# Two-block transformer on one core: order of VectorE's work in the first layer, and half a weight unit more held ahead of the experts

## The chip, the cores and the metric

The kernel runs on one core of one Trainium2 chip. Its time is the device time of one execution in microseconds (us), given as the median of three executions. The trace comes from one further execution. The engines are TensorE (PE, its weight loads are PEld), VectorE (DVE), ScalarE (ACT), GpSimd (POOL) and SyncE (SP), which here issues nearly all transfers from device memory.

## The reference, cut to what matters

All tensors are float32, with 256 tokens of 1024 channels. Two blocks follow each other, and each has two layers. The first layer of the first block (the "even layer") computes attention and a state-space model (SSM) from one projection:

```python
proj = h @ w_in                       # 1024 x 5120
q, k, v, g_att, u_ssm, g_ssm = split(proj)
lam_bar = exp(lam * dt)               # complex, 32 groups x 64 states
states = scan(a_r * s_l + s_r)        # over the 256 tokens
y = real(c_mat @ states) + d_skip * u_ssm
```

Both layers of the second block end in sixteen experts. Every expert picks its 32 tokens:

```python
xn = rms_norm(h, norm2_g)
affinity = softmax(xn @ w_router)
gate, idx = top_k(affinity.T, 32)     # per expert
xe = xn[idx]
hid = silu(xe @ w_gate) * (xe @ w_up) # 32 x 1024 @ 1024 x 1024
ye = (hid @ w_down) * gate
h = h + scatter_add(ye, idx)
```

The weights of one expert are three matrices of 4 MB, 12 MB in all. One layer of experts reads 201 MB, two read 403 MB of the 514 MB that the program reads.

## The kernel before

**Units.** Weights come in units of 2 MB, 16 KB in each of 128 partitions. SP issues one DMA for each in a fixed order, on one queue, and waits before each until the memory it goes to is free. TensorE counts finished units in `unit_done`. A dense weight is multiplied in three products of rounded parts: ACT copies a landed unit to its high part (`high_part`, L866), DVE subtracts that to get the low part (`low_part`, L1220, 128x4096 elements), and only then may TensorE start the unit (L1635 to L1637). Unit numbers in the text are those of this list: the even layer's are 0 to 10.

**Even layer.** TensorE runs each unit in four quarters, and a table written out by hand (`SSM_STEPS`) puts pieces of the SSM ahead of certain quarters. T0 to T3 (L1792, L1795) build the blocks within four tokens and stand ahead of the third and fourth quarter of unit 3. V0 to V3 (L1807) are the drives of the four groups of states. V2 stands ahead of the second quarter of unit 4, V3 ahead of its fourth. V2 writes the bank that the first group's drive was read from, so it waits until DVE's `states(0)` has read it (the second instruction of `states`, L1197). V3 waits in the same way for `states(1)`. DVE has its own written order: after the powers (`cpow_ready`, a memset at L1265) come `low_part(4)`, eight `whole_block` (L1272, they read what T0 and T1 made), the angles (L1280 to L1291: turns, fractions and the step table), `states(0)`, `low_part(5)`, `states(1)`, and eight more `whole_block`. T2 and T3 reuse the banks of T0 and T1 and wait for the first and the second four `whole_block`. ACT takes the sines of the angles (`sincos`, L825) between the high parts of units 4 and 5. POOL rotates q and k meanwhile (L689 to L694).

**Experts.** An expert is six units: j = 0 to 3 are gate and up, 4 and 5 are down (96 in a layer). There are six places in `ring` and four in `board`. Nine of them form a wheel, and the tenth takes the unit j = 9 (`ONCE`) alone. So ten units are asked for before the first one has been used. Of the unit j = 10 (`HALVED`), the first half (1 MB) goes to `row_half` early. The second half goes to the place of unit j = 0, so it waits until TensorE has done that unit (L615). From then on SP waits for one finished unit ahead of each transfer.

**Ahead of the experts.** The router's scores come to DVE and ACT at the end of each layer's output projection. ACT takes the exponentials (`lg_exp`, L1054). DVE multiplies `x` by 1/rms into `xs` (the first token tile in `normalise(0)`, the second at L1520), finds the 32 best tokens of each expert (L1524 to L1529), and compares the ranks with 0 to 31 (L1532) for `csel`, a one-hot matrix of the first expert. TensorE's `gather` (L2157) multiplies `csel` by `xs` to pick the rows, and DVE's `choose` (L1561) makes `csel` for the expert after the next.

Of the kernel before, what the change touches and what calls it, by code (L numbers as in the profile page):

```python
# [26 lines left out]
ALU = mybir.AluOpType  # L27
# [3 lines left out]
P = 128  # L31
S = 256
D = 1024
NT = S // P
# [19 lines left out]
ONCE = WHEEL  # L54
HEAD_E = 2

HALVED = 10
# [3 lines left out]
def wheel_place(j):  # L61

    return j if j < ONCE else (j - ONCE - 1) % WHEEL


def extra_slot(j):

    return EXTRA - 1 if j == ONCE else EXTRA_OF.get(wheel_place(j))
# [105 lines left out]
def build(nc, a, out):  # L174

    with ExitStack() as ctx:
# [21 lines left out]
        row = row_half[:, 0:D]  # L198
        vec = sb("vec", [P, NVEC])
# [136 lines left out]
        csel = next_area("p (i c) -> p i c", i=NT, c=CAP)  # L336
        wselT = next_area("p (i s) -> p i s", i=NT, s=P)
# [64 lines left out]
        user, place, high_place, slot_no, count_in, loads = [], [], [], [], [], [0] * (RING + EXTRA)  # L402
# [165 lines left out]
        half_in = sem("half_in")  # L568
# [18 lines left out]
        def _(sp):  # L587
# [13 lines left out]
            for l in range(2):  # L601
# [6 lines left out]
                def load_moe(e, j, turn=None):  # L608
# [5 lines left out]
                    elif j > ONCE:  # L614
                        sp.wait_ge(unit_done, u - (WHEEL if j - ONCE > WHEEL else WHEEL + 1) + 1)  # L615
# [8 lines left out]
                    if turn is None and j == HALVED:  # L624
                        src = down[e, :, 1, :, :].rearrange("p b n -> p (b n)")
                        sp.dma_start(slot_mem(s)[:, SLOT // 2:SLOT], src).then_inc(landed[s], 16)
                        return
# [21 lines left out]
                for j in range(6 * (HEAD_E + TURN_E)):  # L649
                    if j not in (2, 3):  # L650
                        load_moe(j // 6, j)
                    if j == 1:
                        sp.wait_ge(rot_done, 8 * (l + 1))
                        sp.dma_start(row_half[:], down[HALVED // 6, :, 0, :, :].rearrange("p b n -> p (b n)")).then_inc(half_in, 16)
# [416 lines left out]
        def _(dve):  # L1071
# [203 lines left out]
            low_part(4)  # L1275
            for t in range(8):
                whole_block(t)
# [16 lines left out]
            own.settle()  # L1294
            states(0)
            low_part(5)
            states(1)
# [91 lines left out]
            for l in range(2):  # L1389
# [119 lines left out]
                normalise(0)  # L1509
# [22 lines left out]
                tt(csel, slot_in[:, :, 0:1].to_broadcast([P, NT, CAP]), cn("slots").unsqueeze(1).to_broadcast([P, NT, CAP]),  # L1532
                   ALU.is_equal).then_inc(csel_sb, 1)
# [83 lines left out]
        def _(pe):  # L1617
# [351 lines left out]
            for l in range(2):  # L1969
# [178 lines left out]
                count["xs"] += 2 * NT  # L2148

                def gather(e):  # L2150

                    if isinstance(e, int) and e == 0:
                        pe.wait_ge(xs_ready, count["xs"])
# [15 lines left out]
                def expert(e, j0, turn=None, more=True):  # L2169
# [33 lines left out]
                    for j in range(2):  # L2203
                        w = in_place(4 + j)
                        for qq in range(2):
                            for b in range(2):
                                q = 2 * j + qq
                                ahead_half = turn is None and j0 + 4 + j == HALVED and qq == 0
                                if ahead_half and b == 0:
                                    pe.wait_ge(half_in, 16 * (l + 1))  # L2210
                                if not more and j == 1 and qq + b > 0:
                                    pe.wait_ge(tail_in[2 * qq + b - 1], 16 * (l + 1))
                                for r in range(4):
                                    at = qq * 2 * FF + b * FF + 256 * r
# [80 lines left out]
```

## Time and profile before

| | us |
|---|---|
| median of 3 executions | 1670.78 |
| lowest, highest | 1669.49, 1671.78 |
| profiled execution, its own time | 1668.02 |
| span of its trace | 1666.1 |

The span runs from the first to the last instruction, and 1.9 us of the profiled execution's time lie around it. TensorE is busy for 1315.2 us of the span (79%), DVE for 560.9, ACT for 453.5 and POOL for 125.8. The granted TensorE clock is 0.931 of full speed over the span. The DMA engines move 516.56 MB. In the forty slices of the page one slice is 41.7 us: the first eleven are the first block, then come the second block's two layers, each a dense stretch and a stretch of experts (from about 600 to 1033 us, and from about 1222 to 1656 us).

### The profile page before, as it was taken

To read this page: it belongs to the slowest core of one execution; us is meant where nothing else is said; L and a number is where in the kernel's file an instruction comes from. 1 tells how busy PE (TensorE), PEld (TensorE's weight loads), DVE (VectorE), ACT (ScalarE), POOL (GpSimd) and SP (SyncE) were. 2 spreads that over 40 slices of the span, in tenths; PEclk is the share of its full clock that TensorE was granted. 3 is DMA by queue.
4 is the path that set the end of the run, shared out by engine and by line. 5 is a ranking of instruction groups with operands and counts; after the bars stand their busy time and mean duration, and the time that the engine had idled before them with its cause. 6 is when DMAs were issued, how large, how long until landed. Compare 5 with 4: busy or idle time off the path is not lost.

```text
span 1666.1 us, 28296 instructions
## 1 busy us (share of the span) xinstructions
PE 1315.2 (79%) x12544; PEld 925.8 (56%) x12544; DVE 560.9 (34%) x810; ACT 453.5 (27%) x581; POOL 125.8 (8%) x152
## 2 busy tenths in 40 slices
PE   7999999999999987666656565999987666566664
PEld 6888877998888853323223223788853222233222
DVE  7993675355576530000000001485520000000001
ACT  5346555443654311100001011554311101001011
POOL 0320000000305000000000000305000000000000
PEclk9999999999999999988988887999999888988887
DMA  8234343464444799999999999444899999999997
GB/s 284 102 127 141 126 162 125 169 217 168 152 152 178 308 406 423 426 428 424 428 424 428 426 424 410 144 145 179 331 403 424 425 427 426 427 424 427 426 426 310
DMA packets 87104, 516.56 MB, mean 310 GB/s; under 512 B 6513, under 2 KB 6641, under 8 KB 54513
## 3 DMA queue, kind: packets, MB, share of 16 engines
q1 hardware_dynamic: 83520, 509.20, 75.3%
q0 software_dynamic: 992, 3.42, 0.6%
q10 hardware_dynamic: 2512, 2.75, 0.5%
q8 instruction: 66, 1.08, 0.3%
q14 instruction: 14, 0.11, 0.0%
HBM read 514.30 MB, written 1.05 MB: 309 GB/s over the span
## 4 chain that ended last, share of the span: by engine, by line
DMA 46%; PE 39%; DVE 9%; issue 2%; ACT 2%; SPq 2%; DVEq 0%; ACTq 0%
DMA board<-in_w_gate 12%; DMA board<-in_w_down 11%; DMA ring<-in_w_gate 10%; PE dense L1635 8%; PE dense L1637 8%; PE dense L1636 8%; DMA ring<-in_w_down 6%; DMA ring<-in_w_up 5%; PE bank L2185 3%; PE bank L2215 2%; DVE ring_parts L1220 1%; SPq L637 1%; DVE board L1444 1%; PE dense L1688 1%; PE dense L1652 1%
## 5 line engine op out<-in xcount | busy, mean ns | idle before, releaser
L2185 PE MATMUL bank<-ring,board 128*32 128x256 f32 x2624 | 199.5, 458 | 147.1 <-DMA ring<-in_w_up 85.8
L2185 PEld LDWEIGHTS bank<-ring,board 128*32 128x32 f32 x2624 | 91.8, 126 | 248.6 <-DMA ring<-in_w_up 105.3
L1220 DVE TENSOR_TENSOR ring_parts<-ring,ring_parts 128x4096 fp32r<-128x4096 f32 (+1 forms) x44 | 184.5, 4198 | 104.8 <-ACT ring_parts L866 104.6
L1058 ACT ACTIVATE board<-bank 128x256 f32<-128x256 f32 x32 | 12.3, 385 | 740.6 <-PE bank L2185 740.6
L1551 DVE TENSOR_TENSOR board<-board,bank 128x256 f32<-128x256 f32 x32 | 13.5, 422 | 555.9 <-ACT board L1058 555.9
L866 ACT ACTIVATE ring_parts<-ring 128x4096 fp32r<-128x4096 f32 (+1 forms) x48 | 165.1, 3441 | 125.4 <-DMA ring<-in_w_in 39.3
L2185 PE MATMUL bank<-board 128*32 128x256 f32 x1472 | 105.6, 439 | 65.9 <-DMA board<-in_w_up 40.5
L1635 PE MATMUL dense<-board_parts,ring_parts 128*128 128x256 f32 x528 | 152.2, 288 | 0.0
L1637 PE MATMUL dense<-board_parts,ring_parts 128*128 128x256 f32 x528 | 149.4, 283 | 0.0
L1635 PE MATMUL dense<-ring_parts,board_parts 128*128 128x512 f32 x320 | 128.5, 401 | 0.0
L1636 PE MATMUL dense<-ring_parts,board_parts 128*128 128x512 f32 x320 | 124.8, 390 | 0.0
L2215 PE MATMUL bank<-ring,board 128*32 128x256 f32 x1312 | 85.5, 405 | 49.3 <-DMA ring<-in_w_down 42.9
L2185 PEld LDWEIGHTS bank<-board 128*32 128x32 f32 x1472 | 49.4, 123 | 120.3 <-DMA board<-in_w_up 51.3
L1636 PE MATMUL dense<-board_parts,ring_parts 128*128 128x256 f32 x400 | 113.1, 283 | 0.0
L1637 PE MATMUL dense<-ring_parts,board_parts 128*128 128x512 f32 x272 | 106.1, 390 | 0.0
L1635 PEld LDWEIGHTS dense<-board_parts,ring_parts 128*128 128x128 f32 x528 | 101.2, 192 | 1.2 <-issue 0.9
L1637 PEld LDWEIGHTS dense<-board_parts,ring_parts 128*128 128x128 f32 x528 | 101.2, 192 | 0.0
L730 POOL TENSOR_TENSOR board<-board 128x128 f32<-128x128 f32 x64 | 24.3, 400 | 914.0 <-PE bank L2193 772.3
L2215 PEld LDWEIGHTS bank<-ring,board 128*32 128x32 f32 x1312 | 41.3, 115 | 85.9 <-DMA ring<-in_w_down 52.0
L1556 DVE COPY board<-bank 128x256 f32<-128x256 f32 x32 | 13.6, 425 | 221.1 <-PE bank L2215 221.1
L1636 PEld LDWEIGHTS dense<-board_parts,ring_parts 128*128 128x128 f32 x400 | 76.7, 192 | 0.5 <-issue 0.2
L2215 PE MATMUL bank<-board 128*32 128x256 f32 x704 | 48.5, 421 | 28.7 <-DMA board<-in_w_down 25.1
(338 smaller groups left out, 2066.4 us busy)
## 6 DMA issues: line engine op xcount, KB each, us to landing
ring<-in_w_gate SPq DMA_DIRECT2D x42, 2048.0 KB, 40.8
ring<-in_w_up SPq DMA_DIRECT2D x40, 2048.0 KB, 40.8
ring<-in_w_down SPq DMA_DIRECT2D x40, 2048.0 KB, 40.9
board<-in_w_up SPq DMA_DIRECT2D x24, 2048.0 KB, 41.1
board<-in_w_gate SPq DMA_DIRECT2D x22, 2048.0 KB, 41.0
board<-in_w_down SPq DMA_DIRECT2D x20, 2048.0 KB, 40.9
ring<-in_w_in SPq DMA_DIRECT2D x18, 2048.0 KB, 7.9
ring<-in_even_w_in SPq DMA_DIRECT2D x10, 2048.0 KB, 8.3
```

The source lines that it names most:

```text
L637: sp.dma_start(dst, src).then_inc(tail_in[n - 1] if n else landed[s], 16)
L730: g.tensor_tensor(wsel[:, i], csel[:, i:i + 1, :].to_broadcast([P, 4, CAP]), aff[:, i, bass.ds(e, 1)].unsqueeze(2).to_broadcast([P, 4, CAP ...
L866: s.activation(slot_of(u, True)[0], slot_of(u), ACT.Copy).then_inc(hi_done, 1)
L1220: tt(lo, slot_of(u), hi.bitcast(F32), ALU.subtract).then_inc(lo_done, 1)
L1444: tt(qv, qv, by, ALU.mult).then_inc(lv_ready, 1)
L1635: mm(o, x_parts[0], y_parts[0], start=start, stop=False)
L1636: mm(o, x_parts[0], y_parts[1], start=False, stop=False)
L1637: return mm(o, x_parts[1], y_parts[0], start=False, stop=stop)
L1652: last = mm(d[:, i, :], act_T[:, k, i, :], w[:, k, :], start=k == 0, stop=k == nk - 1)
L1688: last = mm(d[:, c // 2, (c % 2) * S:(c % 2 + 1) * S], w[:, k, c * P:(c + 1) * P], act_T[:, k, :], start=k == 0, stop=k == nk - 1)
L2185: last = mm(WB[0][32 * q:32 * q + 32, 256 * (j % 2):256 * (j % 2) + 256], xeT[:, 4 * (j // 2) + k, :], w[:, k * D + 256 * q:k * D + 256 * ...
L2215: last = mm(WB[3][32 * r:32 * r + 32, 0:256], hidT[:, b, 32 * q:32 * q + 32], (row_half if ahead_half else w)[:, at:at + 256], start=q == ...
```

## The change

Four things change, none of them in what is computed.

1. In the even layer DVE's order becomes: angles, eight `whole_block`, `low_part(4)`, `states(0)`, `states(1)`, `low_part(5)`, then as before.
2. The gather reads `x` instead of `xs`. The 1/rms is put into the one-hot matrix: `cselr` is `csel` with `rstd` in place of the ones. The normalisation of `x` into `xs` ahead of the experts goes.
3. The memory of `xs` (1 MB) is free then, and takes the second half of unit j = 10, from the moment that the router's exponentials are done. Unit j = 11 is now the first on the wheel, and waits for unit j = 0; the units 11 to 18 each wait for the unit one earlier than before, 19 for one two earlier, and those from 20 on wait as before.
4. `choose` makes `cselr` as well as `csel`, with one instruction more for each token tile.

```diff
-HALVED = 10
+ONCE, HALVED = WHEEL, WHEEL + 1
 def wheel_place(j):
-    return j if j < ONCE else (j - ONCE - 1) % WHEEL
+    return j if j < ONCE else (j - HALVED - 1) % WHEEL
 def extra_slot(j):
-    return EXTRA - 1 if j == ONCE else EXTRA_OF.get(wheel_place(j))
+    return {ONCE: EXTRA - 1, HALVED: EXTRA}.get(j, EXTRA_OF.get(wheel_place(j)))
...
+        half_mem = [row_half[:], xs[:].rearrange("p i n -> p (i n)")]
...
-                    elif j > ONCE:
-                        sp.wait_ge(unit_done, u - (WHEEL if j - ONCE > WHEEL else WHEEL + 1) + 1)
+                    elif j > HALVED:
+                        sp.wait_ge(unit_done, u - (WHEEL if j - HALVED > WHEEL else WHEEL + 2) + 1)
...
-                    if j not in (2, 3):
+                    if j not in (2, 3, HALVED):
                         load_moe(j // 6, j)
-                    if j == 1:
-                        sp.wait_ge(rot_done, 8 * (l + 1))
-                        sp.dma_start(row_half[:], down[HALVED // 6, :, 0, :, :].rearrange("p b n -> p (b n)")).then_inc(half_in, 16)
+                    if j in (1, ONCE):
+
+                        sp.wait_ge(*((rot_done, 8 * (l + 1)) if j == 1 else (lg_exp, 2 * (l + 1))))
+                        n = int(j == ONCE)
+                        sp.dma_start(half_mem[n], down[HALVED // 6, :, n, :, :].rearrange("p b n -> p (b n)")).then_inc(half_in[n], 16)
...
-            low_part(4)
-            for t in range(8):
-                whole_block(t)
             turns = lambda f: cs[:, f, :].rearrange("p (t b) -> p t b", t=SSM_TILES)
...
             own.settle()
+            for t in range(8):
+                whole_block(t)
+            low_part(4)
             states(0)
+            states(1)
             low_part(5)
-            states(1)
             for t in range(8, SSM_TILES):
                 whole_block(t)
...
-                normalise(0)
+                inverse(0)
...
-                ts(xs[:, 1, :], x[:, 1, :], rstd[:, 1:2], None, ALU.mult).then_inc(xs_ready, 2)
...
-                tt(csel, slot_in[:, :, 0:1].to_broadcast([P, NT, CAP]), cn("slots").unsqueeze(1).to_broadcast([P, NT, CAP]),
-                   ALU.is_equal).then_inc(csel_sb, 1)
+                own.link(tt(csel, slot_in[:, :, 0:1].to_broadcast([P, NT, CAP]),
+                            cn("slots").unsqueeze(1).to_broadcast([P, NT, CAP]), ALU.is_equal))
+                tt(cselr, csel, rstd[:].unsqueeze(2).to_broadcast([P, NT, CAP]), ALU.mult).then_inc(csel_sb, 1)
...
                     dve.wait_ge(wsel_sb, e * 2 + 2 * NE * l)
+                    for i in range(NT):
+                        stt(cselr[:, i, :], cn("slots"), slot[:, i, bass.ds(e, 1)], rstd[:, i:i + 1].to_broadcast([P, CAP]),
+                            ALU.is_equal, ALU.mult)
...
-                            last = mm(WB[3][32 * q:32 * q + 32, 256:512].rearrange("p (b m) -> p b m", b=2), csel[:, i, :],
-                                      xs[:, i, :].rearrange("p (m q b) -> p q b m", q=4, b=2)[:, q], start=i == 0,
+                            last = mm(WB[3][32 * q:32 * q + 32, 256:512].rearrange("p (b m) -> p b m", b=2), cselr[:, i, :],
+                                      x[:, i, :].rearrange("p (m q b) -> p q b m", q=4, b=2)[:, q], start=i == 0,
```

VectorE in the even layer, from the end of the powers (L1265). Before, the low part of unit 4 (L1220) comes first, then the eight blocks (L1272), then the angles (from L1280):

```order
L1265 MEMSET stat 128x1
L1220 TENSOR_TENSOR ring_parts<-ring,ring_parts 128x4096
L1272 SCALAR_TENSOR_TENSOR xs<-con,skip,bank 128x128 x8
L1280 TENSOR_TENSOR board<-con,row_half 128x1024
L1282 TENSOR_SCALAR board<-board 128x1024
L1283 TENSOR_SCALAR row_half<-board 128x1024
```

And now, the same place (the angles are L1277 to L1288):

```order
L1265 MEMSET stat 128x1
L1277 TENSOR_TENSOR board<-con,row_half 128x1024
L1279 TENSOR_SCALAR board<-board 128x1024
L1280 TENSOR_SCALAR row_half<-board 128x1024
L1281 TENSOR_SCALAR board<-board 128x1024
L1282 TENSOR_SCALAR row_half<-row_half 128x1024
L1283 TENSOR_SCALAR board<-board 128x1024
L1284 TENSOR_TENSOR board<-board,row_half 128x1024
L1286 TENSOR_TENSOR board<-board 128x1024
L1288 TENSOR_TENSOR row_half<-row_half,con 128x1024
L1272 SCALAR_TENSOR_TENSOR xs<-con,skip,bank 128x128 x8
L1220 TENSOR_TENSOR ring_parts<-ring,ring_parts 128x4096
```

The low part of unit 4 has moved behind the angles and the blocks.

VectorE at the end of `states(0)` (L1208, L1209). Before, the low part of unit 5 stands between it and `states(1)` (from L1196):

```order
L1208 TENSOR_TENSOR board<-board 128x256
L1209 TENSOR_TENSOR board<-board 128x256
L1220 TENSOR_TENSOR ring_parts<-ring,ring_parts 128x4096
L1196 TENSOR_TENSOR board<-bank,board 128x512
L1197 TENSOR_TENSOR board<-bank,board 128x512
L1200 TENSOR_TENSOR board<-board 128x256
```

And now:

```order
L1208 TENSOR_TENSOR board<-board 128x256
L1209 TENSOR_TENSOR board<-board 128x256
L1196 TENSOR_TENSOR board<-bank,board 128x512
L1197 TENSOR_TENSOR board<-bank,board 128x512
L1200 TENSOR_TENSOR board<-board 128x256
L1201 TENSOR_TENSOR board<-board 128x256
L1204 SCALAR_TENSOR_TENSOR board<-row_half,board 128x256 x2
L1206 TENSOR_TENSOR board<-board 128x512
L1207 TENSOR_TENSOR board<-board 128x512
L1208 TENSOR_TENSOR board<-board 128x256
L1209 TENSOR_TENSOR board<-board 128x256
L1220 TENSOR_TENSOR ring_parts<-ring,ring_parts 128x4096
```

`states(1)` follows `states(0)` at once, and the low part of unit 5 comes after both.

SyncE ahead of the experts. Before, from the unit j = 7 on; the row of 128x2048 elements is the second half of unit j = 10:

```order
L643 DMA ring<-in_w_up 128x4096
L643 DMA ring<-in_w_gate 128x4096
L643 DMA board<-in_w_up 128x4096
L626 DMA ring<-in_w_down 128x2048
L643 DMA ring<-in_w_down 128x2x2048
L643 DMA board<-in_w_gate 128x4096
```

And now:

```order
L641 DMA ring<-in_w_up 128x4096
L641 DMA ring<-in_w_gate 128x4096
L641 DMA board<-in_w_up 128x4096
L654 DMA xs<-in_w_down 128x2048
L641 DMA ring<-in_w_down 128x2x2048
L641 DMA ring<-in_w_gate 128x4096
```

The half unit keeps its place in the queue, but goes to `xs`, and its wait is for the exponentials instead of for unit j = 0.

## Rows read from the trace of the kernel before

**Rows 1.** The page: the chain that ended last, by engine.
```profile
DMA 46%; PE 39%; DVE 9%; issue 2%; ACT 2%; SPq 2%; DVEq 0%; ACTq 0%
```

**Rows 2.** Stretches: busy us of each engine (count), then granted clock, DMA share, GB/s.
```profile
604.50:612.50 8.00, 7.74 (x120) 3.98 (x112) 0.85 (x2) 0.85 (x3) 0.25 (x1) 1.00 0.84 306
612.50:1031.00 418.50, 269.66 (x3470) 129.72 (x3474) 25.73 (x73) 36.64 (x63) 11.11 (x30) 0.88 1.01 425
1226.50:1234.50 8.00, 7.91 (x124) 4.05 (x115) 0.85 (x2) 0.67 (x3) 0.15 (x1) 1.00 0.89 286
1234.50:1652.00 417.50, 271.70 (x3462) 130.24 (x3466) 26.00 (x73) 36.70 (x64) 11.81 (x31) 0.87 1.01 425
```

**Rows 3.** Timeline of TensorE, 77 to 98 us: start, us, engine, line, idle before.
```profile
77.00 0.28 PE L1792 MATMUL bank<-con,xs 128*32 128x32 f32 x3
...
83.48 0.39 PE L1635 MATMUL dense<-ring_parts 128*128 128x512 f32 x1
...
86.25 2.00 PE L1807 MATMUL bank<-board 128*128 128x64 f32 x16
...
96.21 2.00 PE L1807 MATMUL bank<-board 128*128 128x64 f32 x16 [2.43 <-DVE board L1197]
98.02 0.48 PE L1635 MATMUL dense<-ring_parts 128*128 128x512 f32 x1
```

**Rows 4.** Timeline of VectorE, 65 to 96 us.
```profile
65.77 0.06 DVE L1265 MEMSET stat<- 128x1 f32 x1
68.81 4.42 DVE L1220 TENSOR_TENSOR ring_parts<-ring,ring_parts 128x4096 fp32r<-128x4096 f32 x1 [2.98 <-ACT ring_parts L866]
73.15 2.18 DVE L1272 SCALAR_TENSOR_TENSOR xs<-con,skip,bank 128x128 f32<-128x128 f32 x8
75.25 1.22 DVE L1280 TENSOR_TENSOR board<-con,row_half 128x1024 f32<-128x1024 f32 x1
...
84.91 0.69 DVE L1196 TENSOR_TENSOR board<-bank,board 128x512 f32<-128x512 f32 x1
...
90.53 4.42 DVE L1220 TENSOR_TENSOR ring_parts<-ring,ring_parts 128x4096 fp32r<-128x4096 f32 x1
94.87 0.68 DVE L1196 TENSOR_TENSOR board<-bank,board 128x512 f32<-128x512 f32 x1
95.47 0.68 DVE L1197 TENSOR_TENSOR board<-bank,board 128x512 f32<-128x512 f32 x1
```

**Rows 5.** Timeline of GpSimd: first rotation of q, beside L1220 and beside L1272.
```profile
69.78 3.79 POOL L689 TENSOR_TENSOR rtmp<-board,con 128x128 f32<-128x128 f32 x1 [56.78 <-ACT board L787]
73.53 0.45 POOL L690 TENSOR_TENSOR rtmp<-board,con 128x128 f32<-128x128 f32 x1
```

**Rows 6.** Timeline of VectorE, `states(2)`, beside the rotation of k.
```profile
111.71 1.63 DVE L1204 TENSOR_TENSOR_SCAN board<-row_half,board 128x256 f32<-128x256 f32 x2
```

**Rows 7.** Timeline of SP's queue at the start of the experts.
```profile
590.56 0.33 SPq L643 DMA_DIRECT2D board<-in_w_up  x1
604.67 0.33 SPq L626 DMA_DIRECT2D ring<-in_w_down  x1
```

**Rows 8.** Stretches of half a microsecond behind the issue at 604.67.
```profile
604.50:605.00 0.50, 0.50 (x16) 0.32 (x12) 0.00 (x0) 0.00 (x0) 0.00 (x0) 1.00 0.24 98
...
607.00:607.50 0.50, 0.50 (x16) 0.31 (x12) 0.00 (x0) 0.00 (x0) 0.00 (x0) 1.00 1.05 442
```

**Rows 9.** Timeline of VectorE and TensorE ahead of the first gather.
```profile
592.26 0.75 DVE L1520 TENSOR_SCALAR xs<-x,rstd 128x1024 f32<-128x1024 f32 x1
...
598.71 0.23 DVE L1532 TENSOR_TENSOR board<-bank,con 128x64 f32<-128x64 f32 x1 [0.39 <-PE bank L2146]
...
599.09 0.65 PE L2157 MATMUL bank<-xs,board 128*32 128x256 f32 x4 [0.41 <-DVE board L1532]
```

**Rows 10.** Timeline: `choose(1)` on VectorE, and the gather that reads it.
```profile
602.54 0.21 DVE L1561 TENSOR_TENSOR board<-board,con 128x64 f32<-128x64 f32 x1
609.61 2.02 PE L2157 MATMUL bank<-xs,board 128*32 128x256 f32 x16
```

More of the change, by code:

```diff
@@ L51 @@
 TURN_E = 3
-ONCE = WHEEL
+ONCE, HALVED = WHEEL, WHEEL + 1
 HEAD_E = 2
-HALVED = 10
 EXTRA_OF = {2: 2, 3: 1, 4: 0}
 def wheel_place(j):
-    return j if j < ONCE else (j - ONCE - 1) % WHEEL
+    return j if j < ONCE else (j - HALVED - 1) % WHEEL
 def extra_slot(j):
-    return EXTRA - 1 if j == ONCE else EXTRA_OF.get(wheel_place(j))
+    return {ONCE: EXTRA - 1, HALVED: EXTRA}.get(j, EXTRA_OF.get(wheel_place(j)))
 SLOT = 4096
@@ L336, in build @@
         csel = next_area("p (i c) -> p i c", i=NT, c=CAP)
+        cselr = next_area("p (i c) -> p i c", i=NT, c=CAP)
         wselT = next_area("p (i s) -> p i s", i=NT, s=P)
@@ L401, in build @@
         LAST_X = 10
-        user, place, high_place, slot_no, count_in, loads = [], [], [], [], [], [0] * (RING + EXTRA)
+        user, place, high_place, slot_no, count_in, loads = [], [], [], [], [], [0] * (RING + EXTRA + 1)
         extras = []
@@ L567, in build @@
         final_done = sem("final_done")
-        half_in = sem("half_in")
+        half_in = [sem(f"half_in{n}") for n in range(2)]
         tail_in = [sem(f"tail_in{n}") for n in range(3)]
@@ L623, in load_moe @@
                         sp.wait_ge(unit_done, free_at(place[u]))
[L624 to L627, printed above, removed]
                     j = j % 6
@@ L2147, in _ @@
                 last.then_inc(slot_ps, 1)
-                count["xs"] += 2 * NT
                 def gather(e):
-                    if isinstance(e, int) and e == 0:
-                        pe.wait_ge(xs_ready, count["xs"])
                     pe.wait_ge(csel_sb, e + (NE * l + 1))
@@ L2203, in expert @@
                     for j in range(2):
-                        w = in_place(4 + j)
+                        halves = turn is None and j0 + 4 + j == HALVED
+                        w = None if halves else in_place(4 + j)
                         for qq in range(2):
@@ L2207, in expert @@
                                 q = 2 * j + qq
-                                ahead_half = turn is None and j0 + 4 + j == HALVED and qq == 0
-                                if ahead_half and b == 0:
-                                    pe.wait_ge(half_in, 16 * (l + 1))
+                                if halves and b == 0:
+                                    pe.wait_ge(half_in[qq], 16 * (l + 1))
                                 if not more and j == 1 and qq + b > 0:
@@ L2213, in expert @@
                                 for r in range(4):
-                                    at = qq * 2 * FF + b * FF + 256 * r
+                                    at = (0 if halves else qq * 2 * FF) + b * FF + 256 * r
                                     last = mm(WB[3][32 * r:32 * r + 32, 0:256], hidT[:, b, 32 * q:32 * q + 32],
-                                              (row_half if ahead_half else w)[:, at:at + 256], start=q == 0 and b == 0, stop=q == 3 and b == 1,
+                                              (half_mem[qq] if halves else w)[:, at:at + 256], start=q == 0 and b == 0, stop=q == 3 and b == 1,
                                               skip_group_check=True)
```

## The prediction

> **What bounds the kernel now.** I read the chain of waits first. It is 46% transfers, 39% TensorE and 9% VectorE [rows 1]: the kernel has dense stretches, where TensorE sets the time, and expert stretches, where the weights do. So each part of the change has to be valued by the bound of its own stretch.
>
> In the expert stretches the table of windows shows 425 GB/s over 418.5 and 417.5 us, and TensorE busy for about 65% of them [rows 2]. The transfers are the bound there, and a microsecond in which they stand still before the stretch ends is lost for good. Just ahead of each of these windows there are 8 us with only 306 and 286 GB/s [rows 2]. At 425 GB/s those bytes need 8 x 306/425 = 5.8 us and 8 x 286/425 = 5.4 us: 2.2 and 2.6 us are lost there. The reason stands in SP's queue. The last of the ten units asked for in advance is issued at 590.56, the next transfer waits for TensorE's first unit and is issued at 604.67 [rows 7]. By then the queue has run dry: 98 GB/s right behind the issue, and 442 only at 607.0 [rows 8].
>
> In the even layer I looked for places where TensorE stands still. In the stretch that the change touches there is one: V3 (L1807 at 96.21) waited 2.43 us for DVE's L1197 [rows 3]. DVE had begun `states(1)` at 94.87, behind the low part of unit 5, which began at 90.53 [rows 4].
>
> The profiled execution took 1668.02 us, of which 1666.1 are span. The median is 1670.78. I work out a difference from the trace and take it off both.
>
> **Part 1, the even layer.** The same instructions run in another order, so I lay DVE's durations end to end, from the rows of VectorE [rows 4]:
> - Powers end at 65.83. DVE then stood idle for 2.98 us, for ACT's high part of unit 4. The angles need nothing of ACT's and take 84.91 - 75.25 = 9.66 us: they end at 75.5.
> - Eight blocks, 75.25 - 73.15 = 2.10 us: 77.6. The first four are done at 76.5, and T2 is due at 77.00 [rows 3]: 0.5 us to spare.
> - `low_part(4)`, 94.87 - 90.53 = 4.34 us: 81.9. Unit 4 is due on TensorE at 83.48 [rows 3]: 1.5 us to spare.
> - `states(0)`, 90.53 - 84.91 = 5.62 us: 87.6. Its L1197 ends 1.3 us in, at 83.2, and V2 is due at 86.25.
> - `states(1)`: 93.2. Its L1197 ends at 88.9. V3 is due at 96.21 - 2.43 = 93.78: the wait of 2.43 us is gone, with 4.9 us to spare.
> - `low_part(5)`: 97.5, 3 us later than before. Unit 5 is due at V3's start plus V3 (98.02 - 96.21 = 1.81) plus a quarter (86.25 - 83.48 = 2.77): 93.78 + 4.58 = 98.4. This is what is late next, with 0.8 us to spare.
>
> Behind that DVE waits for ACT, which waits for TensorE, and all moves up together. So the gain is 2.4 us. The bounds are 2.5 from one side (the whole wait and a little from V2, which had no slack: L1197 of `states(0)` had ended at 84.91 + 1.3 = 86.2 and V2 began at 86.25) and 0.5 from the other (the next rival). I take 2.4.
>
> **Part 2, half a unit more ahead.** The half (1.05 MB) needs 1.05/0.425 = 2.46 us of the queue. It is now issued once the exponentials are done, which was before 592.26 [rows 9], some 12 us before the queue runs dry. What is left to move after the restart is 1.05 MB less. So the stretch would end 2.46 us earlier if the restart came at the same time.
>
> The restart still waits for TensorE's first unit, and this comes later by the new multiply for `cselr`. The nearest row is L1532, 128x64 elements in 0.23 us [rows 9], and it must wait for `csel` to be written: 0.25 us between L1532 and the gather at 599.09. I charge 0.25, with bounds of 0.2 and 0.5. Gain: 2.46 - 0.25 = 2.2 us in each layer of experts. A cap is the time lost in the dip, 2.2 and 2.6 us, which allows it. The queue would now run dry at 604.5 + 2.46 = 607.0, and what is issued at 604.9 flows from about 607.0 by the same delay as before [rows 8]: it meets just so. If a remnant of the dip stays, 0.5 us goes. Bounds for each layer: 2.5 and 1.2.
>
> Here a page of the Trainium skill can be weighed. "DMA: Bandwidth & Descriptors", section "Latency and other measured facts", puts the first byte of a transfer issued by SyncE about 0.6 us behind its issue. The rows show 98 GB/s right behind the issue and the full rate 2.3 us behind it, so the measurement decides. By the page's figure no remnant could stay, since the new transfer would have 1.5 us in hand; the sum would be the same 2.2, and the lower bound would move up to it.
>
> **Edits that I cost at nothing.** The normalisation of the first token tile lay while DVE had idle time, and L1520 (0.75 us, [rows 9]) while the affinities were being transposed; the chain that follows starts at the same time, give or take 0.1 us. The gather reads `x` in the pattern in which it read `xs`, so it costs the same. `choose` gets two more small instructions for each expert. The nearest row is L1561, 0.21 us, at 602.54, and the gather that needs it is at 609.61 [rows 10]: some 6.9 us of cover where TensorE is the bound, and more later, when it waits for weights. Uncovered, two of them would cost 0.42 us for each of 32 experts, 13.4 us in all. The rotated wheel makes the next layer's first dense units wait for one expert unit more. They still stand behind undelivered weights in the queue, so this costs nothing.
>
> **Sum.** 2.4 + 2.2 + 2.2 = 6.8 us: 1668.0 - 6.8 = 1661.2 for a profiled execution like this one, and 1670.8 - 6.8 = 1664.0 for the median.
>
> **Rivals.**
> - *The wait moves to unit 5 (15%).* DVE works from 65.8 to 97.5 without a pause, and the end has 0.8 us to spare. POOL rotates q in this time. Beside L1220 its first instruction took 3.79 us, beside the blocks 0.45 [rows 5]; and the two scans of `states(2)` took 1.63 us beside POOL [rows 6]. For it: with L1220 now later, the rotation can end inside `states(0)`. If that stretches DVE by 1.5 to 2.7 us, unit 5 starts 0.7 to 1.9 us late, and the even layer gives 0.5 to 1.7 instead of 2.4: 1665.3 at 1.1. Against it: only one or two of POOL's twelve instructions should be left. The Trainium skill speaks for this rival: "SBUF — State Buffer", section "SBUF: two separate sides", has the port pair shared by VectorE and GpSimd as an exclusive lock, so that the other fully blocks. The rows of POOL agree with that.
> - *The dip stays (15%).* The queue runs dry anyway, and the slow start behind it comes again, so that each layer gives 1.0 instead of 2.2: 1670.8 - 2.4 - 2.0 = 1666.4. For it: the meeting at 607.0 has no slack. Against: the bytes are moved ahead in any case.
> - *The half unit doesn't help (4%).* It would do this if TensorE, not the weights, set the pace after the restart. Then only part 1 is left: 1668.4. Against it stands the steady 425 GB/s with TensorE at 65% [rows 2].
> - *Slower (3%).* `choose` comes onto the path. Its place is between the input of one expert and the gather of the next. It decides from the point at which DVE ends `choose` later than TensorE reaches that gather, so when the 6.9 us of cover are used up, and from there each expert pays its 0.42 us: 1670.8 - 6.8 + 13.4 = 1677.4. Nothing in the rows comes near that point.
>
> **How the numbers follow.** The forecast holds 63%: 1664.0, and with the bounds of its terms (0.4 less in the even layer, 0.5 less in each layer of experts; 0.7 more in all) 1663.3 to 1665.4. The first two rivals lie at 1665.3 and 1666.4. The median of three differs by about 1 us from one set to another (1669.49 to 1671.78 before). So the range is 1661.8 to 1668.0, and leaves out the last two rivals and the tails. 0.2%, or 3.3 us, is about what a measurement of this kernel can tell from no change. Faster by more than that: the forecast, nearly all of the first rival, most of the second, 0.88 in all. Within it: the third, the rest of the second, 0.09. Slower: 0.03.
>
> **What would show it.** In the even layer: no idle time ahead of V3, DVE without a pause from the powers to the second eight blocks, and unit 5 not waiting for L1220. If unit 5 waits, the first rival holds. In the experts: the transfer into `xs` issued near 590 us (the even layer's gain already taken off), no stretch of 98 GB/s at the restart, and the 8 us around it near 400 GB/s. The gather 0.25 us later behind L1528 than it was behind L1529. The last weight lands about 2.2 us earlier in the first layer of experts, beyond the even layer's gain, and about 4.4 us in the second. I am wrong if the dip is filled and the end doesn't move, since then the transfers are not the bound that I take them for.

## The result, and the profile after

| | us |
|---|---|
| changed kernel, median of 4 executions | 1661.13 (1660.33 to 1663.90) |
| kernel before, 4 executions beside them | 1670.48 (1669.49 to 1671.78) |
| ratio, 95% interval | 0.9948 [0.9936, 0.9960] |
| predicted | 1664.0, range 1661.8 to 1668.0 |

The change saves 9.35 us where 6.8 were predicted, and the time lies 0.7 us below the range. Two more comparisons of the same kernel (below) gave 0.9936 and 0.9944. The mean of the three ratios is 0.9943, or 9.6 us. The interval of this first comparison (6.7 to 10.7 us) still just takes in the forecast of 6.8. The intervals of the two others do not (8.4 to 12.9 and 7.0 to 11.7), so the gain was too small in the prediction, and this is hardly chance. One execution of before in the sets below took 1885 us at a granted clock of 0.69, and is left out of the comparisons.

The profiled execution of the changed kernel took 1663.90 us. That is only 4.1 less than the profiled execution of before (1668.02), less than half of what the medians show. Before's was 2.5 under its median, this one is 2.8 above its own. It began late: the powers end at 68.1 instead of 65.8 [rows 4]. In its trace TensorE stands idle for 2.16 us ahead of them, within the small matmuls of L1765 (here L1768), without a wait that the profile shows ("issue"):

```profile
38.34 0.31 PE L1768 MATMUL bank<-board,con 32*32 32x64 f32 x7 [2.16 <-issue]
```

The trace of before has no such gap. So I read steps in these two traces, and sizes in the medians.

The chain of waits of the changed kernel (the page):

```profile
DMA 45%; PE 43%; DVE 8%; issue 2%; ACT 2%; SPq 0%; DVEq 0%; ACTq 0%
```

SP's 2% have gone from it [rows 1]. TensorE in the even layer, by timeline (start, us, engine, line, idle before):

```profile
89.33 1.89 PE L1810 MATMUL bank<-board 128*128 128x64 f32 x16
96.61 1.89 PE L1810 MATMUL bank<-board 128*128 128x64 f32 x16
98.31 0.48 PE L1638 MATMUL dense<-ring_parts 128*128 128x512 f32 x1
```

V3 (at 96.61) has no idle time ahead of it, where it had 2.43 us [rows 3]. VectorE in the same stretch:

```profile
68.00 1.22 DVE L1277 TENSOR_TENSOR board<-con,row_half 128x1024 f32<-128x1024 f32 x1
...
76.58 2.16 DVE L1272 SCALAR_TENSOR_TENSOR xs<-con,skip,bank 128x128 f32<-128x128 f32 x8
78.65 4.42 DVE L1220 TENSOR_TENSOR ring_parts<-ring,ring_parts 128x4096 fp32r<-128x4096 f32 x1
82.99 0.69 DVE L1196 TENSOR_TENSOR board<-bank,board 128x512 f32<-128x512 f32 x1
...
84.38 0.67 DVE L1200 TENSOR_TENSOR board<-board 128x256 f32<-128x256 f32 x1
...
89.72 0.68 DVE L1197 TENSOR_TENSOR board<-bank,board 128x512 f32<-128x512 f32 x1
90.51 0.43 DVE L1200 TENSOR_TENSOR board<-board 128x256 f32<-128x256 f32 x1
...
94.73 4.42 DVE L1220 TENSOR_TENSOR ring_parts<-ring,ring_parts 128x4096 fp32r<-128x4096 f32 x1
```

This is the chain that the prediction laid end to end, without a pause, 2.2 us later at its start and 1.6 us at its end. The angles take 76.58 - 68.00 = 8.6 us instead of the 9.66 that were read from the trace of before. L1197 of `states(1)` ends at 90.4, 6.2 us ahead of V3. The low part of unit 5 ends at 99.15, and unit 5 is due a quarter (2.77 us, the prediction's figure) behind 98.31, so 1.9 us later. The first rival's stretching shows, but is small: `states(0)` takes 89.11 - 82.99 = 6.1 us instead of 5.6 [rows 4], since some of its instructions run beside GpSimd: its L1200 takes 0.67, and that of `states(1)` takes 0.43.

The start of the experts, in windows of 8 us around the restart of the queue and then the stretches behind them (columns as in [rows 2]), changed kernel:

```profile
604.00:612.00 8.00, 8.00 (x124) 4.18 (x116) 0.84 (x2) 0.57 (x2) 0.00 (x0) 1.00 0.96 373
1224.00:1232.00 8.00, 8.00 (x140) 4.33 (x132) 0.42 (x1) 0.38 (x1) 0.00 (x0) 1.00 0.97 382
612.00:1029.00 417.00, 272.57 (x3479) 130.34 (x3482) 30.10 (x101) 36.95 (x64) 11.32 (x30) 0.87 1.01 425
1232.00:1650.00 418.00, 269.90 (x3486) 130.81 (x3484) 30.62 (x102) 37.09 (x64) 11.92 (x31) 0.88 1.00 424
```

306 and 286 GB/s have become 373 and 382, and the steady rate stays at 425. What the dip loses falls from 2.2 and 2.6 us to 8 - 8 x 373/425 = 1.0 and 0.8 us. Another profile of the same kernel (the run "the changed kernel again" below) has still less of it:

```profile
602.30:610.30 8.00, 7.98 (x124) 3.88 (x116) 0.85 (x2) 0.60 (x2) 0.01 (x1) 1.00 1.01 423
1220.90:1228.90 8.00, 7.96 (x124) 4.09 (x116) 0.85 (x2) 0.63 (x2) 0.10 (x1) 1.00 1.02 420
```

The stretch ahead of the first gather, first SP's queue and then VectorE and TensorE:

```profile
591.30 0.33 SPq L654 DMA_DIRECT2D xs<-in_w_down  x1
604.45 0.38 SPq L641 DMA_DIRECT2D ring<-in_w_down  x1
```

```profile
598.05 0.23 DVE L1531 TENSOR_TENSOR board<-bank,con 128x64 f32<-128x64 f32 x1 [0.39 <-PE bank L2149]
598.31 0.23 DVE L1533 TENSOR_TENSOR board<-board,rstd 128x64 f32<-128x64 f32 x1
...
598.59 0.67 PE L2157 MATMUL bank<-x,board 128*32 128x256 f32 x4 [0.58 <-DVE board L1533]
```

The half unit is asked for 13 us ahead of the restart. From the start of the making of `csel` to the gather it was 0.38 us [rows 9], and is 0.54 now: `cselr` costs 0.16 us, not 0.25.

### The profile page after: what moved, and what is told of

Same layout as the page of the kernel before. It is cut to its first block, busy times and chain, and to the rows that moved or that the text cites. A ratio compares the mean times of both kernels' runs of the same rounds, so it can differ in the third digit from the quotient of the medians.

```text
span 1662.1 us, 28385 instructions
## 1 busy us (share of the span) xinstructions
PE 1315.4 (79%) x12544; PEld 928.1 (56%) x12544; DVE 567.2 (34%) x866; ACT 453.8 (27%) x581; POOL 125.2 (8%) x152
## 3 DMA queue, kind: packets, MB, share of 16 engines
HBM read 514.30 MB, written 1.05 MB: 310 GB/s over the span
## 4 chain that ended last, share of the span: by engine, by line
DMA 45%; PE 43%; DVE 8%; issue 2%; ACT 2%; SPq 0%; DVEq 0%; ACTq 0%
DMA board<-in_w_down 21%; DMA board<-in_w_gate 15%; PE dense L1638 9%; PE dense L1640 8%; PE dense L1639 8%; DMA board<-in_w_up 5%; PE bank L2185 4%; PE bank L2215 3%; DMA ring<-in_w_up 2%; DVE ring_parts L1220 1%; DMA ring<-in_even_w_in 1%; PE dense L1655 1%; DVE board L1444 1%; DVE board L1435 1%; PE bank L2010 1%
## 5 line engine op out<-in xcount | busy, mean ns | idle before, releaser
L2185 PE MATMUL bank<-ring,board 128*32 128x256 f32 x2688 | 211.2, 470 | 152.2 <-DMA ring<-in_w_up 90.5
L1220 DVE TENSOR_TENSOR ring_parts<-ring,ring_parts 128x4096 fp32r<-128x4096 f32 (+1 forms) x44 | 184.3, 4193 | 105.2 <-ACT ring_parts L866 105.1
L2185 PE MATMUL bank<-board 128*32 128x256 f32 x1408 | 101.2, 440 | 60.1 <-DMA board<-in_w_up 35.5
L2215 PE MATMUL bank<-ring,board 128*32 128x256 f32 x1280 | 77.3, 383 | 50.0 <-DMA ring<-in_w_down 44.7
L1638 PE MATMUL dense<-ring_parts 128*128 128x512 f32 (+1 forms) x192 | 67.8, 353 | 1.3 <-DVE ring_parts L1220 1.3
```

The lines of the kernel that those rows point to most:

```text
L1220: tt(lo, slot_of(u), hi.bitcast(F32), ALU.subtract).then_inc(lo_done, 1)
L1638: mm(o, x_parts[0], y_parts[0], start=start, stop=False)
L2185: last = mm(WB[0][32 * q:32 * q + 32, 256 * (j % 2):256 * (j % 2) + 256], xeT[:, 4 * (j // 2) + k, :], w[:, k * D + 256 * q:k * D + 256 * ...
L2215: last = mm(WB[3][32 * r:32 * r + 32, 0:256], hidT[:, b, 32 * q:32 * q + 32], (half_mem[qq] if halves else w)[:, at:at + 256], start=q == ...
```

## The experiments

All ratios are to the kernel before, run beside on the same chip, five rounds each, with 95% intervals. Three sets of four kernels each had their own executions of before: median 1670.56 for the first four, 1669.52 for the next four (the kernel before again, the filled wait, only `states(1)` moved, the half unit late), 1670.44 for the last four. Gains in us are worked out from the ratio, and can differ by about 1 us from the difference of the medians.

**The even layer's order alone.** The kernel before, with only the new order of VectorE:

```diff
-            low_part(4)
-            for t in range(8):
-                whole_block(t)
...
+            for t in range(8):
+                whole_block(t)
+            low_part(4)
             states(0)
-            low_part(5)
             states(1)
+            low_part(5)
```

> The kernel before with VectorE's new order in the even layer alone (angles, blocks, low part of unit 4, both first states, low part of unit 5). Theory A (the forecast's terms are right, and what was measured beyond 6.8 us is spread between executions): 2.4 us faster than before, ratio 0.9986, and no idle time ahead of V3. Theory B (the even layer's term is mis-sized and holds the missing 2.5 us): 4 to 5 us faster. Theory C (the experts' terms hold it): 2.4 us faster here as well, so A and C are told apart by the run with the experts' part alone.

Measured: 1665.90 us, 0.9970 [0.9961, 0.9979], 5.0 us less (3.5 to 6.5). The forecast of 2.4 lies below the interval.

**The experts' part alone.** The changed kernel, with before's order in the even layer:

```diff
+            low_part(4)
+            for t in range(8):
+                whole_block(t)
...
-            for t in range(8):
-                whole_block(t)
-            low_part(4)
             states(0)
-            states(1)
             low_part(5)
+            states(1)
```

> The changed kernel with VectorE's old order in the even layer, so that only the experts' part is changed. Theory A: 4.4 us faster than before (2.2 in each layer of experts). Theory B: the same 4.4. Theory C: 6 to 7 us faster, more than the 2.46 us a layer that the half unit takes on the queue, so something beside the moved bytes gains.

Measured: 1666.12 us, 0.9977 [0.9968, 0.9987], 3.8 us less (2.2 to 5.3). The forecast of 4.4 lies inside. So the excess is in the even layer.

**The gather from `x` alone.** The kernel before, with `cselr` and the gather that reads `x`, but the half unit where it was:

```diff
-                normalise(0)
+                inverse(0)
...
+                tt(cselr, csel, rstd[:].unsqueeze(2).to_broadcast([P, NT, CAP]), ALU.mult).then_inc(csel_sb, 1)
...
-                            last = mm(WB[3][...], csel[:, i, :],
-                                      xs[:, i, :]...
+                            last = mm(WB[3][...], cselr[:, i, :],
+                                      x[:, i, :]...
```

> The kernel before with the gather from x and the scaled one-hot matrix, without the further half unit (its second half still goes to the wheel after the first unit). Theory A: 0.25 us later at the first gather of each layer of experts, so 0 to 0.5 us slower than before, within what can be told. Theory C in the form that reading x or dropping the normalisation is itself a gain: 2 us or more faster than before.

Measured: 1671.24 us, 1.0007 [0.9998, 1.0016], 1.2 us more (0.3 less to 2.7 more). It gains nothing by itself. The price worked out from the rows, 0.16 us twice, lies inside.

**The changed kernel again**, in the same set.

> The changed kernel once more, on the same chip and against the same runs of before. Theory A: 6.8 us faster (ratio 0.9959), closer to the forecast than the first measurement's 9.35. Theories B and C: 9 us faster again (ratio 0.9945), and the runs of the two parts alone then show which of them holds more than its term.

Measured: 1659.88 us, 0.9936 [0.9923, 0.9950], 10.7 us less (8.4 to 12.9). The parts add up within their intervals: 5.0 + 3.8 = 8.8.

**The kernel before again.** In the first two of these traces TensorE's clock looked otherwise than in the profiled execution of before, so this run is a second look at the kernel before.

> The kernel before once more, for a second profile of it and as a measure of what a null change shows. Clock theory (TensorE's granted clock falls to half for some 6 us after its wait of 2.43 us ahead of V3, in most executions but not in the profiled one that the prediction was made from, and that costs 3 us beyond the wait): ratio within 0.998 to 1.002, and the profile shows granted clock 0.5 for about 6 us from 97 us on, with 63 to 64 us from T0 to the last piece of the SSM on TensorE instead of 60.5. Rival (the first profile is typical, the clock fell in the profiles of the other runs by chance): no fall there, 60.5 us.

Measured: 1670.23 us, 1.0005 [0.9996, 1.0014]: the same time. But the trace is not the same. First the window from 98 to 104 us of the profiled execution that the prediction was made from, then of this one (the column behind POOL is the granted clock):

```profile
98.00:104.00 6.00, 6.00 (x31) 5.01 (x30) 4.54 (x13) 3.90 (x2) 0.00 (x0) 1.00 0.29 75
```

```profile
98.00:104.00 6.00, 6.00 (x20) 5.13 (x20) 5.32 (x14) 1.02 (x1) 0.00 (x0) 0.50 0.01 3
```

The granted clock is at 2.4 GHz in the one and at 1.2 GHz in the other, and 20 instructions fit where 31 did. The timeline of TensorE in the second execution:

```profile
87.03 2.00 PE L1807 MATMUL bank<-board 128*128 128x64 f32 x16
...
96.99 2.95 PE L1807 MATMUL bank<-board 128*128 128x64 f32 x16 [2.42 <-DVE board L1197]
99.70 0.77 PE L1635 MATMUL dense<-ring_parts 128*128 128x512 f32 x1
100.27 0.63 PE L1636 MATMUL dense<-ring_parts 128*128 128x512 f32 x1
...
107.57 0.33 PE L1821 MATMUL bank<-board,xs 128*128 128x64 f32 x2
```

And where the same last row stands in the execution of the prediction:

```profile
103.59 0.33 PE L1821 MATMUL bank<-board,xs 128*128 128x64 f32 x2
```

Ahead of V3 stands the same wait, 2.42 us instead of 2.43. Behind it V3 takes 2.95 us instead of 2.00 [rows 3], and a matmul of 128x512 elements 0.63 instead of 0.40. From the start of V3 to L1821 it is 107.57 - 96.99 = 10.58 us here and 103.59 - 96.21 = 7.38 there: the fall costs 3.2 us. The two other kernels with the old order and this wait, the experts' part alone and the gather from `x` alone, have the same fall:

```profile
98.00:104.00 6.00, 6.00 (x20) 5.13 (x20) 5.07 (x14) 1.02 (x1) 0.00 (x0) 0.50 0.01 3
```

```profile
98.00:104.00 6.00, 6.00 (x22) 5.23 (x22) 5.73 (x15) 1.02 (x1) 0.00 (x0) 0.50 0.01 3
```

With the new order there is no wait and no fall. The changed kernel, and then the even layer's order alone:

```profile
98.00:104.00 6.00, 6.00 (x31) 5.02 (x31) 3.23 (x9) 3.61 (x2) 0.00 (x0) 1.00 0.21 50
```

```profile
98.00:104.00 6.00, 6.00 (x32) 5.10 (x32) 3.73 (x9) 3.13 (x2) 0.00 (x0) 1.00 0.17 29
```

So three of four profiles with the wait ahead of V3 have the fall, and the prediction was made from the fourth. All seven profiles in which TensorE waits neither for V3 nor for unit 5 (those of the changed kernel, of the even layer's order, of the angles alone, of the half unit late and of the further zeroing) stay at 2.4 GHz there.

**The wait kept, with TensorE busy in it.** The kernel before, with fifteen multiplications by zeros ahead of V3's wait. They add zeros to a bank, and the result stays what it was.

```diff
+                if c == 3:
+                    for _ in range(15):
+                        mm(DP[0][:, 1, 0:96], ident, cn("none"), start=False, stop=False, skip_group_check=True)
```

> The kernel before, VectorE's order unchanged, with 15 small matmuls on TensorE ahead of V3. They add zeros to the running sum of unit 4 (stationary identity, moving 96 columns of zeros), so that TensorE works while it waits for VectorE. V3 starts no earlier than before. Clock theory: no fall of the clock behind V3, about 3 us faster than before (ratio 0.998) although the wait for VectorE is as long as ever. Rival (the missing time is in VectorE's order or in the weights, not in the clock): the same as before, or 0.1 to 0.5 us slower.

Measured: 1668.31 us, 0.9990 [0.9981, 0.9999], 1.7 us less (0.2 to 3.2). The medians lie 1.2 us apart. The timeline of TensorE shows the wait filled (L1805; the 15 multiplications stand in it as 30 records), and V3 later than before:

```profile
94.08 3.49 PE L1805 MATMUL dense<-con 128*128 128x96 f32 x30
97.40 0.47 PE L1810 MATMUL bank<-board 128*128 128x64 f32 x3
...
104.66 0.33 PE L1824 MATMUL bank<-board,xs 128*128 128x64 f32 x2
```

The clock stays at 2.4 GHz:

```profile
98.00:104.00 6.00, 6.00 (x34) 5.17 (x34) 4.99 (x14) 2.83 (x2) 0.00 (x0) 1.00 0.13 12
```

From V3 to L1824 it is 7.26 us, as without the fall. In this profile V2 starts at 86.69, so V3 starts 97.40 - 86.69 = 10.71 us behind it, where it was 96.99 - 87.03 = 9.96: the zeros hold V3 back by 0.75 us. Work that computes nothing and moves V3 back still makes the kernel faster. A wait has a second price here, the clock behind it.

**Only `states(1)` ahead of `low_part(5)`.** The kernel before, with the angles left behind the low part of unit 4:

```diff
             states(0)
-            low_part(5)
             states(1)
+            low_part(5)
```

> The kernel before with only states(1) moved ahead of the low part of unit 5, and the angles left behind the low part of unit 4. Laid end to end, VectorE then ends the low part of unit 5 at 100.5 us of the first trace, where TensorE is due for it at 98.4. Clock theory: the wait of 2.4 us ahead of V3 goes, one of 2 us ahead of unit 5 comes, and the clock falls behind that one, so the gain is 0 to 1 us. Rival (the pause ahead of V3 alone matters): 5 us faster, like the whole new order.

Measured: 1669.44 us, 0.9994 [0.9984, 1.0003]: not to be told from before. The wait has moved to unit 5, and the fall with it. Its timeline of TensorE, and its window behind that wait:

```profile
103.25 0.76 PE L1635 MATMUL dense<-ring_parts 128*128 128x512 f32 x1 [2.39 <-DVE ring_parts L1220]
```

```profile
103.00:107.00 4.00, 3.75 (x10) 3.01 (x11) 4.00 (x10) 2.85 (x2) 0.00 (x0) 0.57 1.04 401
```

**Only the angles and blocks ahead of `low_part(4)`.** The kernel before, with the other half of the new order:

```diff
-            low_part(4)
-            for t in range(8):
-                whole_block(t)
...
+            for t in range(8):
+                whole_block(t)
+            low_part(4)
             states(0)
             low_part(5)
             states(1)
```

> The kernel before with the angles and the eight blocks moved ahead of the low part of unit 4, and the low part of unit 5 left between the two first states. Laid end to end, VectorE's L1197 of states(1) ends at 93.2 us of the first trace, and TensorE comes to V3 at 93.8. Clock theory (what counts is that TensorE isn't kept waiting, since the clock falls behind the wait): no wait ahead of V3, no fall of the clock behind it, and the whole 5 us of the even layer, ratio 0.997, although half of the reordering is missing. Rival (both moves share the gain): 2 to 3 us faster.

Measured: 1664.88 us, 0.9963 [0.9950, 0.9976], 6.2 us less (4.0 to 8.4). Its timelines of VectorE and TensorE:

```profile
92.43 0.68 DVE L1197 TENSOR_TENSOR board<-bank,board 128x512 f32<-128x512 f32 x1
```

```profile
93.49 0.33 PE L1807 MATMUL bank<-board 128*128 128x64 f32 x2
```

L1197 ends at 93.1, just ahead of V3, which doesn't wait. So moving the angles does all of the work that can be measured, and the swap of `states(1)` and `low_part(5)` adds nothing that shows. The interval (of five executions) overlaps with that of the whole order.

**The pause put back.** The changed kernel, in which V3 also waits for the low part of unit 5:

```diff
+                if c == 3:
+                    pe.wait_ge(lo_done, vector_lows(5))
```

> The changed kernel with one wait more: TensorE holds V3 until VectorE has made the low part of unit 5, which is 3.8 us after it comes to V3. Nothing else is changed, and the same work is done. Clock theory: the wait costs its 3.8 us, the granted clock is at half for some 6 us behind it, which costs 3 us more, so this kernel is 6 to 7 us slower than the changed kernel and 3 us faster than before. Rival (a wait costs only its length): 3.8 us slower than the changed kernel, 6 us faster than before.

Measured: 1665.20 us, 0.9969 [0.9960, 0.9979]. By the ratios this is 4.2 us slower than the changed kernel in the same set, by the medians 2.1, and the two intervals together leave some 3 us of doubt on either side. The timeline of TensorE, and the window behind it:

```profile
99.27 0.99 PE L1812 MATMUL bank<-board 128*128 128x64 f32 x7 [2.47 <-DVE ring_parts L1220]
```

```profile
100.00:105.00 5.00, 5.00 (x22) 4.29 (x22) 1.28 (x5) 1.02 (x1) 0.00 (x0) 0.66 0.01 3
```

The wait is 2.47 us long, not the 3.8 expected. In the trace it is 8.96 us from V3's start to L1826, where the changed kernel needs 7.27 to the same instruction (L1824), so here the fall (3.4 us at half clock) costs 1.7. Wait and fall add up to 2.5 + 1.7 = 4.2 us. The measured difference agrees with this, but it does not rule out the rival by itself, by which 2.5 us would be lost: it is the trace that shows the second price. I had expected more, since I had counted on the longer fall of the kernel before.

**The half unit late.** The changed kernel, in which the half unit waits for TensorE's first expert unit, as it did before:

```diff
-                        sp.wait_ge(*((rot_done, 8 * (l + 1)) if j == 1 else (lg_exp, 2 * (l + 1))))
+                        sp.wait_ge(*((rot_done, 8 * (l + 1)) if j == 1 else (unit_done, MOE[l] + 1)))
```

> The changed kernel, but the second half of unit j = 10 is asked for into the memory of xs only when TensorE has done its first expert unit, at the restart. Theory that the experts' gain is the megabyte moved ahead of the restart: the dip of 2 us around the restart is back in both layers and the 4.4 us are lost, so this kernel is 5 us faster than before (the even layer's part alone) and 4 to 5 us slower than the changed kernel. Rival (the gain comes from the wheel that begins one unit later, or from the free xs): as fast as the changed kernel, 9 to 10 us faster than before.

Measured: 1665.56 us, 0.9976 [0.9965, 0.9987], 4.0 us less than before, which is about what the even layer gives alone. The windows around the restart:

```profile
604.40:612.40 8.00, 8.00 (x128) 3.88 (x116) 0.85 (x2) 0.50 (x2) 0.00 (x0) 1.00 0.82 312
1225.60:1233.60 8.00, 8.00 (x128) 3.88 (x116) 0.85 (x2) 0.48 (x2) 0.00 (x0) 1.00 0.82 318
```

The dip is back, 2.1 and 2.0 us are lost again, and the gain of the experts is gone. It hangs on when that megabyte is asked for, not on the gather or the memory.

**More work ahead of the first gather.** The changed kernel with four zeroing products instead of three where the ranks are waited for:

```diff
-                zero(3).then_inc(gt_ps, 1)
+                zero(4).then_inc(gt_ps, 1)
```

> The changed kernel with 16 instead of 12 of the matmuls that clear the output banks while VectorE picks the tokens, so that TensorE waits less just ahead of the first gather. Clock theory: the fall of the clock in the first expert (598 to 601 us and 1219 to 1223 us in the changed kernel's profile) becomes rarer, the restart of the weights comes up to 0.5 us earlier, and the kernel is 0 to 1 us faster than the changed kernel. Rival (weights bound, the restart is met by the further half unit anyway): the same as the changed kernel, within 0.5 us.

Measured: 1661.62 us, 0.9947 [0.9934, 0.9960], no different from the changed kernel. Its one profile has no fall behind the first gather, but a longer one ahead of it (10.2 us at half clock between 587 and 598 us), so the question of that clock is not settled.

**The changed kernel a third time**, in that set.

> The changed kernel for the third time, as the measure for the other three of this set on the same chip. Clock theory with the experts' term as forecast: 5 us from the even layer and 4.4 from the experts, 9 to 10 us faster than before (ratio 0.994 to 0.9945), and its profile shows no fall of the clock behind V3.

Measured: 1663.09 us, 0.9944 [0.9930, 0.9958], 9.4 us less (7.0 to 11.7). Its profile shows no fall behind V3.

## Why the prediction was wrong, point by point

**The step that failed** is the last one of part 1: "So the gain is 2.4 us", with a bound of 2.5 from above. The mechanism was right, the size was not: the even layer's order gives 5.0 us alone (3.5 to 6.5). I valued the wait at its own length. But in three of four profiles TensorE's clock falls to half behind it, and the fall costs 3.2 us more.

The traces show the size too. From V2's start to the first instruction of the SSM behind unit 4 (L1821, L1824 in the changed kernel) TensorE needs:

| | us |
|---|---|
| before, the profile of the prediction: 103.59 - 86.25 | 17.34 |
| before again, with the fall: 107.57 - 87.03 | 20.54 |
| changed kernel: 103.88 - 89.33 | 14.55 |

So the new order saves 2.8 us without the fall (the wait and 0.4 more: V2 and V3 each take 0.1 less, and the quarters between them the rest), which is already over the bound of 2.5, and 6.0 with it. If the fall comes in three executions of four, which is an estimate from four profiles, the mean is 2.8 + 0.75 x 3.2 = 5.2. That the fall belongs to the wait is shown by the traces (seen with the wait, never without) and by the filled wait, which takes away the fall and keeps V3 late, and is faster. The wait put back brings the fall back in its trace.

The time of the profiled execution could not have warned me. It lay 2.5 us under the median, but single executions of before run from 1665.6 to 1673.8 us, and the profile of the filled wait, with no fall there either, took 1673.18, 4.9 above its median. What could have warned me stands in the trace of before itself, a wait of 1.70 us of TensorE with a fall behind it:

```profile
255.78 0.70 PE L1665 MATMUL dense<-ring_parts,board_parts 128*128 128x512 f32 x1 [1.70 <-ACT board_parts L781]
256.28 0.63 PE L1666 MATMUL dense<-ring_parts,board_parts 128*128 128x512 f32 x1
```

So the upper bound should not have ended at the length of the wait.

**The experts, 2.2 us a layer.** Right within what can be measured. The part alone gave 3.8 (2.2 to 5.3) for 4.4, and the changed kernel beats the even layer's order by 4.6 us (9.6 - 5.0), or 5.7 in the same set. Over the 20 us from 5 ahead of the restart, a layer loses 2.3 us in the mean of the fourteen layers with the old order of transfers, and 0.5 in the mean of the twelve with the half unit ahead (none in some layers, up to 1.8 in others). A remnant of 0.5 was in the bounds. The runs with the half unit late and with the gather alone show that the gain hangs on the moved megabyte. The forecast that the last weight lands 4.4 us earlier in the second layer can't be read from one pair of traces. From the issue of unit j = 2 to the first addition at a layer's end there are 479.3 us with the old order of transfers (mean of fourteen layers) and 477.5 with the new one (mean of twelve): 1.8 a layer, and single layers of one kind differ by more than 3 us.

**`cselr` at 0.25 us:** 0.16. **`choose` at nothing:** right. Its instructions end at 602.9 in the trace, 6.5 us ahead of the next gather at 609.38.

**The angles at 9.66 us:** 8.6, so there was more room than forecast. Their second instruction (L1282, now L1279) took 0.83 us in the trace of before and takes 0.69 in the changed kernel.

**The rivals.** The wait did not move to unit 5. It does so when the swap is made without the angles. GpSimd stretched `states(0)` by 0.5 us, not 1.5 to 2.7, since most of its rotation had passed: its longest instruction took 4.65 us at 78.74, beside L1220:

```profile
78.74 4.65 POOL L690 TENSOR_TENSOR rtmp<-board,con 128x128 f32<-128x128 f32 x1
...
83.35 0.46 POOL L691 TENSOR_TENSOR rtmp<-board,con 128x128 f32<-128x128 f32 x1
```

The dip did not stay, the half unit did help, and nothing was slower. I had four rivals in which the gain was smaller than forecast and none in which it was larger, and this is why the range ended too high.

**The filled wait, and what is left open.** Filling the wait gave 1.7 us, not the 3 expected. Three falls in four would make 0.75 x 3.2 = 2.4, and from V2's start to L1824 the filled wait needs 104.66 - 86.69 = 17.97 us, 0.6 more than the 17.34 without a fall. That leaves 1.8.

Three things stay open. How often the fall comes is known from four profiles alone. Every one of the fourteen profiles has another fall of 3.4 us, between 247 and 264 us or between 419 and 430 us (one has both), with or without the fall behind V3; this is the trace of before, and then the one with the wait filled:

```profile
255.00:260.00 5.00, 4.22 (x11) 3.31 (x12) 4.36 (x7) 4.74 (x3) 0.00 (x0) 0.66 0.01 3
```

```profile
257.00:261.00 4.00, 4.00 (x11) 3.13 (x12) 3.46 (x5) 3.92 (x2) 0.00 (x0) 0.57 0.00 0
```

What decides its place, no run shows. And the late start with TensorE idle near 36 us stands in seven profiles: in six of the eight with the angles moved ahead, and in one of the six others. Whether the new order brings it, or chance, I did not try; it would be a cost that the medians already contain. No kernel here beats the changed one.

## What to carry to other kernels

A wait of TensorE in a stretch that it bounds is worth its own length plus what the clock gives back, so let the upper bound hold both: here waits of 2.4 us had falls behind them that cost 1.7 or 3.2 us more. Take a second profile of the kernel before pricing a wait, since one execution may lack the fall that others have. And when transfers run dry at a hand-over, memory that is free a little earlier, even for half a unit, is worth up to its bytes at the steady rate (2.5 us here, of which 1.9 a layer were measured).

## What the runs showed of the hardware

- Behind a wait of 2.39 to 2.47 us in an otherwise busy stretch the granted clock fell from 2.4 to 1.2 GHz in five of six profiles, for 3.4 or 6.8 us. The long fall cost 3.2 us, a short one 1.7. Two executions of one kernel, with the same wait at the same place, differ in it.
- The length of a wait does not decide it alone. Behind the wait of 1.2 us that these kernels have between 152 and 162 us, no profile has a fall. Behind one of the waits of 1.1 and 1.7 us that follow each other between 241 and 261 us, ten of fourteen profiles have a fall of 3.4 us.
- In seven of fourteen profiles TensorE stood idle for 1.5 to 2.3 us near 36 us, without a wait that the profile shows. In these the first blocks of the SSM (T0) start at 72.7 to 74.1 us, in the other seven at 70.4 to 71.6.
- Where the queue ran dry ahead of the restart, 1.5 to 3.7 us of its steady rate were lost (mean 2.3 of fourteen layers). With 1.05 MB more asked for ahead, it was 0 to 1.8 us (mean 0.5 of twelve).
